# The last MLP of a two-block float32 kernel: seven block products in place of eight, by quarters of its width

## What is computed

```python
def sqrelu_mlp(h, ln_g, w1, w2):
    u = rmsnorm_2(h, ln_g) @ w1            # 1024x1024 @ 1024x4096
    return jnp.square(jax.nn.relu(u)) @ w2 # 1024x4096 @ 4096x1024

def second_block(...):
        h = h + hybrid_mixer(...)          # ends in a product with w_out
        h = h + sqrelu_mlp(h, ln_ff_g[l], w_ff1[l], w_ff2[l])
    return rmsnorm_2(h, ln_final_g)
```

## Time and profile before

| | us |
|---|---|
| median of 3 runs | 3316.43 (3313.20 to 3319.68) |
| span of the profiled execution | 3317.3 |
| first MATMUL of the MLP starts, in that span | 2424.74 |
| last MATMUL of the MLP starts | 3309.75 |
| last row scaled, its store issued | 3314.56 |

### The profile page before, as it was taken

The page is one execution under the profiler, slowest core; times in us unless marked ns, Lnnn a source line. Parts: engine busy times, 40 slices in busy tenths (PEclk is TensorE's granted clock), DMA queues, the critical chain, the costliest instruction groups (busy, mean ns, idle before and its releaser), DMA issues.

```text
span 3317.3 us, 29920 instructions
## 1 busy us (share of the span) xinstructions
PE 3054.0 (92%) x11898; PEld 1709.6 (52%) x11898; DVE 927.3 (28%) x1752; ACT 616.2 (19%) x1331; POOL 476.0 (14%) x471
## 2 busy tenths in 40 slices
...
DMA packets 195403, 444.93 MB, mean 134 GB/s; under 512 B 27377, under 2 KB 125105, under 8 KB 183089
## 3 DMA queue, kind: packets, MB, share of 16 engines
...
## 4 chain that ended last, share of the span: by engine, by line
PE 64%; DVE 2%; issue 1%; DMA 1%; ACT 1%; POOL 0%; POOLq 0%; SPq 0%; ACTq 0%; DVEq 0%
PE bank L3067 13%; PE bank L3098 13%; PE bank L1942 8%; PE bank L1945 7%; PE bank L2361 5%; PE bank L2940 3%; PE bank L2531 3%; PE bank L2529 2%; PE bank L2863 2%; PE bank L2873 2%; PE bank L232 1%; PE bank L1911 1%; PE bank L2744 1%; PE bank L2741 1%; PE bank L882 1%
## 5 line engine op out<-in xcount | busy, mean ns | idle before, releaser
L3098 PE MATMUL bank<-w_ff,uT 128*128 128x512 f32 x1024 | 441.7, 594 | 3.6 <-DVE hT L3155 3.6
L3067 PE MATMUL bank<-hT,w_ff 128*128 128x512 f32 x1024 | 439.8, 592 | 0.0
L3098 PEld LDWEIGHTS bank<-w_ff,uT 128*128 128x128 f32 x1024 | 195.0, 191 | 250.1 <-issue 243.8
L3067 PEld LDWEIGHTS bank<-hT,w_ff 128*128 128x128 f32 x1024 | 194.4, 190 | 243.9 <-issue 243.9
L489 PE MATMUL bank<-w_in,hT 128*128 128x512 f32 x512 | 224.5, 599 | 3.3 <-DVE hT L401 2.3
L1942 PE MATMUL bank<-e_w,e_xsT 128*128 128x256 f32 x832 | 185.3, 384 | 1.6 <-DVE e_xsT L2027 1.6
L1945 PE MATMUL bank<-e_w,e_xsT 128*64 128x256 f32 x1408 | 164.2, 394 | 19.8 <-issue 19.8
L1942 PEld LDWEIGHTS bank<-e_w,e_xsT 128*128 128x128 f32 x832 | 158.6, 192 | 33.0 <-issue 11.3
L2361 PE MATMUL bank<-w_gla,nT 128*128 128x512 f32 x384 | 167.7, 597 | 1.3 <-ACT nT L2325 1.3
L792 PE MATMUL bank<-hT,w_qkv 128*128 128x512 f32 x384 | 168.8, 598 | 0.0
L489 PEld LDWEIGHTS bank<-w_in,hT 128*128 128x128 f32 x512 | 97.9, 192 | 124.9 <-issue 123.1
...
## 6 DMA issues: line engine op xcount, KB each, us to landing
...
wa<-in_w_ada SPq DMA_DIRECT2D x24, 1024.0 KB, 8.1
...
```

The lines of the kernel that those rows point to most:

```text
L3067: t = pe.matmul(k.bank[2 * (j % 2) + h][:, :], w[:, f, :], hT[:, f, h * BANK:(h + 1) * BANK], start=f == 0, stop=f == NK - 1)
L3098: t = pe.matmul(k.bank[2 * n + h][:, :], b.uT[:, f, m * P:(m + 1) * P], b.ring[j % SLOTS][:, h * BANK:(h + 1) * BANK], start=f == 0, stop= ...
```

## The change

The MLP runs over four quarters of its width of 4096. A quarter has two phases: up (ph even: `hT` by 1024 columns of w_ff1) and down (ph odd: `uT`, 1024 rows of it, by 1024 rows of w_ff2). Each phase is a product of 1024 x 1024 by 1024 x 1024, cut into 2 x 2 blocks of 512; instead of eight block products it makes seven (`STEPS`), from sums and differences of blocks (Winograd's form of Strassen's method). A step is one block product: 4 groups g, each of 4 pairs over f, into 4 of the 8 banks; steps alternate between the two sets of four banks.

Steps 0, 1 and 3 start new sums; steps 2, 4 and 6 go on adding to the banks of step 0, and step 5 to those of step 3. Each step's banks are read after it, before the next step of the same set adds to them (`mlp_taken`, waited for by TensorE per group). In the up phase, ScalarE copies the banks of steps 0, 2 and 3 to `uT` and takes relu of step 6; VectorE adds those of steps 1, 4 and 5 and makes relu and square in one operation, and multiplies for step 6. In the down phase, VectorE adds the banks of every step to the residual rows `x_out`, which now stay in SBUF: the store to DRAM and the load back are gone.

The sums of weight blocks are four GpSimd operations of 128 x 2048 in each phase (`mlp_gpsimd`), the sums of token blocks four VectorE operations of that size (`mlp_sums_vector`): once for `hT`, and in each down phase for `uT`. Six places of 1 MB (`mlp_blocks`) hold four weight blocks and two sums and change roles from phase to phase; SyncE loads four blocks of 1024 KB for each phase.

At the end, tiles 0 to 3 are complete after step 5 of the last phase, and tiles 4 to 7 after step 6, one group each. ScalarE, GpSimd and the stores are as before for each tile. Cut to its core (the bodies removed are printed above; `mlp_areas`, `mlp_signals` and two helpers of a line or two are left out):

```diff
-def out_sync(k, s, b, mlp_s, mlp_b, x_dram, x_out):
+def out_sync(k, s, b, mlp_s, mlp_b, x_dram):
 
     sy = k.nc.sync
     for m, got in enumerate(out_x_got(s)):
         sy.dma_start(b.x[m][:, :], x_dram[m * P:(m + 1) * P, :]).then_inc(*got.up().inc)
-    for j in range(2):
-        mlp_load(k, mlp_s, mlp_b, j)
-    for m in range(NT):
-        if m == NT - 1:
-            sy.wait_ge(*s.out_made(2 * m + 1))
-            for j in range(2, SLOTS):
-                mlp_load(k, mlp_s, mlp_b, j)
-        sy.wait_ge(*s.x_added(2 * (m + 1)))
-        sy.dma_start(x_out[m * P:(m + 1) * P, :], b.x[m][:, :]).then_inc(*s.x_stored.up().inc)
+    for role, tiles in ((0, 0), (1, 0), (2, 2), (3, 3)):
+        if tiles:
+            sy.wait_ge(*s.out_made(2 * tiles))
+        mlp_load(k, mlp_s, mlp_b, 0, role)
...
+QUARTERS = 4
+STEPS = 7
+ROLES = (((0, 0), (1, 0), (0, 1), (1, 1)))
+UP_COPIED, UP_ADDED = (0, 2, 3), (1, 4, 5, 6)
...
+def mlp_blocks(b, ph):
+    slots = list(range(6))
+    for _ in range(ph):
+        b11, b21, b12, b22, e1, e2 = slots
+        slots = [b11, e2, e1, b12, b22, b21]
+    return [b.w[n] for n in slots]
...
+def mlp_taken(s, ph, step, g):
+    q, down = divmod(ph, 2)
+    if down:
+        return s.added(44 * q + 16 + 4 * step + g + 1)
+    if step in UP_COPIED:
+        return s.copied(12 * q + 4 * UP_COPIED.index(step) + g + 1)
+    return s.added(44 * q + 4 * UP_ADDED.index(step) + g + 1)
...
+def mlp_load(k, s, b, ph, role):
...
+    if ph:
+        last, sums = ((0, 3), (2, 4), (3, 0), (4, 0))[role]
+        sy.wait_ge(*mlp_made(s, ph - 1, last))
+        if sums:
+            sy.wait_ge(*s.w_summed(4 * (ph - 1) + sums))
...
+def mlp_operands(b, hT, ph):
+    b11, b21, b12, b22, e1, e2 = mlp_blocks(b, ph)
+    xT, sums = (b.uT, [b.u_sums[0], b.u_sums[1]]) if ph % 2 else (hT, b.h_sums)
+    s4 = quadrant(xT, 0, 0) if ph % 2 else sums[2]
+    tokens = (quadrant(xT, 0, 0), quadrant(xT, 1, 0), sums[1], sums[0], quadrant(xT, 0, 1), s4, quadrant(xT, 1, 1))
+    return tokens, (b11, b21, e2, e1, b12, b22, b21)
...
+def mlp_tensor(k, s, b, out_s, out_b):
     pe = k.nc.tensor
+    for ph in range(2 * QUARTERS):
+        q, down = divmod(ph, 2)
+        tokens, weights = mlp_operands(b, out_b.hT, ph)
+        for step in range(STEPS):
+            mlp_step_waits(k, s, out_s, ph, step)
+            x, w = tokens[step], weights[step]
+            for g in range(4):
+                bank = k.bank[4 * ((ph + step) % 2) + g]
+                if ph == 0 and step == 0:
+                    pe.wait_ge(*out_s.x_added(2 * (NT - 2) + g + 1))
+                elif ph == 0 and step == 1:
+                    if g == 0:
+                        pe.wait_ge(*out_s.half_0_out(4 * NT))
+                        pe.wait_ge(*out_s.half_1_out(4 * NT))
+                elif step < 2:
+                    pe.wait_ge(*mlp_taken(s, ph - 1, STEPS - 2 + step, g))
+                else:
+                    pe.wait_ge(*mlp_taken(s, ph, step - 2, g))
+                part = slice(g * P, (g + 1) * P)
+                for f in range(4):
+                    still, moving = (x[:, f, part], w[:, f, :]) if down else (w[:, f, part], x[:, f, :])
+                    t = pe.matmul(bank[:, :], still, moving, start=step in (0, 1, 3) and f == 0, stop=f == 3, skip_group_check=True)
+                t.then_inc(*s.product_made.up().inc)
+                if ph == 0 and step == 0 and g == 1:
+                    out_turn(k, out_s, out_b, NT - 1)
...
+def mlp_step_waits(k, s, out_s, ph, step):
+    pe, (q, down) = k.nc.tensor, divmod(ph, 2)
+    if ph == 0 and step == 0:
+        pe.wait_ge(*out_s.half_0_out(2 * NT))
+        pe.wait_ge(*out_s.half_1_out(2 * NT))
+    if step in (0, 1):
+        pe.wait_ge(*(s.w_got_0, s.w_got_1)[step](ph + 1))
+        if down:
+            pe.wait_ge(*s.u_ready(12 * q + (4, 12)[step]))
     else:
+        pe.wait_ge(*s.w_summed(4 * ph + (3, 1, 2, 2, 4)[step - 2]))
+        if step < 6:
+            sums = (2, 1, 3, 4)[step - 2]
+            pe.wait_ge(*(s.u_summed(4 * q + sums) if down else s.h_summed(sums)))
...
+def mlp_scalar(k, s, b, x, out):
     a, uT = k.nc.scalar, b.uT
+    for q in range(QUARTERS):
+        ph = 2 * q
+        for step, col, th in ((0, 0, 0), (2, 4, 0), (3, 4, 1)):
+            for g in range(4):
+                a.wait_ge(*mlp_made(s, ph, step, g))
+                src = k.bank[4 * ((ph + step) % 2) + g]
+                a.activation(uT[:, col + g, th * BANK:(th + 1) * BANK], src[:, :], ACT.Copy).then_inc(*s.copied.up().inc)
+        for g in range(4):
+            a.wait_ge(*mlp_made(s, ph, 6, g))
+            a.activation(uT[:, g, BANK:], k.bank[4 * (ph % 2) + g][:, :], ACT.Relu).then_inc(*s.relu_ready.up().inc)
     for at in range(NT):
+        a.wait_ge(*(s.added(44 * QUARTERS - 8 + at + 1)))
         if at:
             a.wait_ge(*s.squared(at))
+        a.activation(b.sq[:, :], x[at][:, :], ACT.Square, scale=D ** -0.5, accum_out=b.ss[:, at:at + 1]).then_inc(*s.squared.up().inc)
         if at < NT // 2:
             a.wait_ge(*s.row_ready(at + 1))
+            a.dma_start(out[0, at * P:(at + 1) * P, :], x[at][:, :]).then_inc(*s.half_stored.up().inc)
     a.wait_ge(*s.half_stored(NT // 2))
...
+def mlp_gpsimd(k, s, b, out_s):
+    g = k.nc.gpsimd
+    for ph in range(2 * QUARTERS):
+        b11, b21, b12, b22, e1, e2 = [x[:, :, :] for x in mlp_blocks(b, ph)]
+        if ph:
+            g.wait_ge(*mlp_made(s, ph - 1, 5))
+        else:
+            g.wait_ge(*out_s.out_made(12))
+        g.wait_ge(*s.w_got_0(ph + 1))
+        g.wait_ge(*s.w_got_2(ph + 1))
+        g.tensor_tensor(e1, b12, b11, ALU.subtract).then_inc(*s.w_summed.up().inc)
+        g.wait_ge(*s.w_got_3(ph + 1))
+        g.wait_ge(*s.w_summed(4 * ph + 1))
+        g.tensor_tensor(b12, b22, b12, ALU.subtract).then_inc(*s.w_summed.up().inc)
+        if ph:
+            g.wait_ge(*mlp_made(s, ph - 1, 6))
+        g.wait_ge(*s.w_summed(4 * ph + 2))
+        g.tensor_tensor(e2, b12, b11, ALU.add).then_inc(*s.w_summed.up().inc)
+        g.wait_ge(*s.w_summed(4 * ph + 3))
+        g.wait_ge(*mlp_made(s, ph, 1))
+        g.tensor_tensor(b21, b21, e2, ALU.subtract).then_inc(*s.w_summed.up().inc)
     for at in range(NT):
+        g.wait_ge(*s.squared(at + 1))
         inverse_root(k, b.ss[:, at:at + 1], s.eps_added, s.rstd)
...
+def mlp_sums_vector(k, xT, s1, s2, s4, summed, first_used):
+    v = k.nc.vector
+    a11, a12, a21, a22 = quadrant(xT, 0, 0), quadrant(xT, 1, 0), quadrant(xT, 0, 1), quadrant(xT, 1, 1)
+    v.tensor_tensor(s1, a21, a22, ALU.add).then_inc(*summed.up().inc)
+    v.wait_ge(*summed.now())
+    v.tensor_tensor(s2, s1, a11, ALU.subtract).then_inc(*summed.up().inc)
+    v.tensor_tensor(a21, a11, a21, ALU.subtract).then_inc(*summed.up().inc)
+    v.wait_ge(*summed.now())
+    if first_used is not None:
+        v.wait_ge(*first_used)
+    v.tensor_tensor(s4, a12, s2, ALU.subtract).then_inc(*summed.up().inc)
...
+def mlp_up_vector(k, s, b, q, step, col, th):
+    v, ph = k.nc.vector, 2 * q
+    for g in range(4):
+        dst, src = b.uT[:, col + g, th * BANK:(th + 1) * BANK], k.bank[4 * ((ph + step) % 2) + g][:, :]
+        v.wait_ge(*mlp_made(s, ph, step, g))
+        if step == 6:
+            v.wait_ge(*s.relu_ready(4 * q + g + 1))
+            m = s.added.up()
+            v.tensor_tensor(dst, dst, src, ALU.mult).then_inc(*m.inc)
+            v.wait_ge(*m)
+            continue
+        v.wait_ge(*s.copied(12 * q + 4 * {1: 0, 5: 1, 4: 2}[step] + g + 1))
+        m = s.added.up()
+        v.tensor_tensor(dst, dst, src, ALU.add).then_inc(*m.inc)
+        v.wait_ge(*m)
+        v.scalar_tensor_tensor(dst, dst, 0.0, dst, ALU.max, ALU.mult).then_inc(*s.u_ready.up().inc)
...
+def mlp_vector(k, s, b, out_s, x, hT):
...
+    for q in range(QUARTERS):
+        if q == 0:
+            v.wait_ge(*out_s.half_0_out(4 * NT))
+            v.wait_ge(*out_s.half_1_out(4 * NT))
+            mlp_sums_vector(k, hT, *(full(t) for t in b.h_sums), s.h_summed, None)
+        for step, col, th in ((1, 0, 0), (4, 4, 1), (5, 4, 0), (6, 0, 1)):
+            mlp_up_vector(k, s, b, q, step, col, th)
+        ph = 2 * q + 1
+        v.wait_ge(*s.u_ready.now())
+        mlp_sums_vector(k, b.uT, full(b.u_sums[0]), full(b.u_sums[1]), quadrant(b.uT, 0, 0), s.u_summed, mlp_made(s, ph, 0))
+        for step, rows, cols in ((0, 0, 0), (1, 0, 0), (2, 0, 1), (3, 1, 1), (4, 1, 1), (5, 0, 1), (6, 1, 0)):
+            if step == 1 or step == 4:
+                v.wait_ge(*mlp_taken(s, ph, step - 1, 3))
+            if q == QUARTERS - 1 and step == 6:
+                v.wait_ge(*s.norm_got(1))
+                for at in range(4):
+                    mlp_row_vector(k, s, b, x, at)
+            for g in range(4):
+                mlp_down_vector(k, s, x, ph, step, rows, cols, g)
+                if q == QUARTERS - 1 and step == 6:
+                    mlp_row_vector(k, s, b, x, 4 + g)
```

(39 more changed lines are left out.)

117 lines of the change are left out of this document (25 added, 92 removed).

## The result

The change took 3218.84 us (3216.17 to 3219.63, 4 runs) against 3314.81 us (3313.12 to 3319.68, 4 runs): ratio 0.970, 95% interval 0.9679 to 0.9721, so 96.0 us less, where 103.4 were forecast; the range of the forecast, 3204 to 3232, holds the new time.

A forecast was written before the change was run, and what follows sets the result against it. TensorE's matmuls, busy 92% of the span, were taken as the bound; -109.9 - 5.2 + 11.7 = -103.4 us took the span from 3317.3 to 3213.9, median 3213 us, own range 3207 to 3220, wider range 3204 to 3232.

The forecast's parts named there:

- Fewer products: TensorE in the MLP: 56 steps of 16 pairs instead of 1024 pairs, at an unchanged price per MATMUL; 109.9 us less.
- The turn in the middle: Between the token halves: TensorE's 3.6 us wait and 1.5 us at a lower clock vanish; 5.2 us less.
- Sums on GpSimd and VectorE: New block sums, 3.8 to 5.7 us each on GpSimd and 2.35 on VectorE, all covered by matmuls; 0 us.
- The two together: GpSimd and VectorE sums in phase 0: even never running side by side, they end 4.4 us before the third product; 0.
- Loads and stores: Weight block loads, landing 8.1 us after issue, are covered; the residual's stores and load back were beside matmuls; 0 gained.
- The clock: Four engines busy together in the MLP would not lower the granted clock of 1.00; 0.
- The end: Last rows after TensorE: tiles 0 to 3 at 3.8 us hold up tiles 4 to 7 at 4.06; 11.7 us more.
- The sum: All terms over the profiled execution: -109.9 - 5.2 + 11.7 = -103.4, span 3213.9, median 3213 us.
- (1): Rival, chance 0.12: TensorE stalls in each phase on a sum, bank or load; at 5 us a phase, 3253.
- (3): Rival, chance 0.03: GpSimd's sums become the bound and the kernel slower; the gain is gone at 17.4 us each.
- (2): Rival, chance 0.05: the end stays short, tiles 0 to 3 not holding up tile 4; 6.1 us behind TensorE, 3204.
- (4): Rival, given no chance: the change makes no fewer instructions on TensorE than counted.

The follow-up runs named there:

- the run with five operations: Against the change's kernel, GpSimd makes the first and third weight sum of each phase twice, five operations ahead of the third product; 3216.36 us.
- the two runs with a wait: Against the change's kernel, GpSimd makes the first and third weight sum of each phase three times (3231.30 us), or twice (3216.36 us).
- the second run on the end: Against the change's kernel, SyncE issues all eight output stores instead of ScalarE issuing some, with VectorE's order kept; 3209.03 us.

## Why the prediction was right, point by point

TensorE's part of the MLP went from 885.6 to 770.1 us, 115.5 less, and the end became 12.0 us longer.

- **Fewer products, -109.9.** Right, and shown: steps of 13.73 us, no idle time, and the eighth product given back costs 109.9. Groups of 4 pairs pay nothing for their boundaries, which the forecast had left open up to 4 us: 27.46 us for 64 MATMULs is 0.429 us each, as before.
- **The turn in the middle, -5.2.** Right, as far as is known: the clock is 1.00 and the wait gone, and 115.5 less the 109.9 leave 5.6. No run puts the turn back, so its size is what is left over.
- **Sums on GpSimd and VectorE, 0.** Right in cost. 31 of GpSimd's 32 sums take 4.5 to 4.8 us, inside the bounds of 3.8 to 5.7; one takes 6.44, over what the forecast called its upper end, because it met VectorE's sums. The Trainium skill's figure (GPSIMD Engine Reference, "Elementwise — side-by-side cycle accounting") is 4497 ns; the trace agrees.
- **The two together, 0 with 4.4 us to spare.** Right that it is hidden. GpSimd's row and VectorE's in the change's phase 0:

```profile
2440.07 6.44 POOL L3178 TENSOR_TENSOR w_ff<-w_ff,w_ff 128x2048 f32<-128x2048 f32 x1
...
2442.17 6.49 DVE L3193 TENSOR_TENSOR h_sum<-h_sum,hT 128x2048 f32<-128x2048 f32 x1
```

  The later of the two ends at 2448.66, due 2457.03: 8.4 us to spare, and 4.4 was the bound with dearer operations. The forecast's 5.7 was too low for a sum in turns and too high for one alone, and only one of the three was in turns for its whole length. That the two take turns is shown by the run with five operations. The Trainium skill (SBUF — State Buffer, "SBUF: two separate sides") has the rule: a VectorE operation with two SBUF inputs and a GpSimd operation that reads SBUF exclude each other for the whole instruction. The trace agrees: 4.51 us alone against 6.43 for GpSimd's sum, 2.29 against 6.49 for VectorE's.
- **Loads and stores, 0.** Right; a 1024 KB block landed 5.2 us after its issue (median). Stores: shown by putting them back. The load back was only argued.
- **The clock, 0.** Right: 1.00 over the whole MLP. It holds while TensorE has no wait; the two runs with a wait lost 1.7 and 1.8 us to it.
- **The end, +11.7.** Right: 16.2 us behind TensorE for 15.9, so +12.0. Tiles 0 to 3 at 3.9 us each for 3.8, tiles 4 to 7 at 4.06.
- **The sum.** 789.1 us for the MLP, 789.0 measured. That it is met to a tenth is partly luck: TensorE's part was 0.4 us shorter than forecast (770.1 for 770.5) and the end 0.3 longer. The rest of the program was taken as fixed, and most of the forecast's distance to the result lies there: the start of the MLP spreads over 10 us, where the range gave 3 us to the runs. The 3213 also came from a span less 0.9, though a span and a run's time are two measures (3217.7 and 3219.63 for the execution profiled after). The medians, 3218.84 and 3214.06, stand 5.8 and 1.1 above 3213 and differ from those before by 96.0 and 102.7 us; 103.6 is what the two MLPs differ by.
- **The rivals.** (1) and (3) fell: no wait of TensorE in any phase. (2) fell: tile 4 was held up. Its 6.1 us behind TensorE need more than ScalarE free of the stores: with these gone (the second run on the end) tile 3's scaling still stood ahead of tile 4's add, and the last scaling ended 8.6 us behind TensorE, where that run's expectation had 7.9. (4) fell with the 1792 MATMULs.
